# A two-layer encoder step on one core: slot releases by halves, reordered loads around the expert stages, and a rearranged start

## The reference, cut to what matters

```python
# layer 0
h = rms_norm(x, g)
proj = h @ w_in                    # 3072 columns + 8 forget columns
fox = softmax attention over 8 heads x 64, logits + cumulative log_sigmoid(forget)
ret = retention, 4 heads (dk 64, dv 128), rotary on q and k, decay per chunk
x = x + concat(fox, silu(gate) * head_norm(ret)) @ w_out
x = x + moe(rms_norm(x, g))
# layer 1
u = glu(rms_norm(x, g) @ w_pw1)    # 2048 columns
y = silu(layer_norm(causal_depthwise_conv31(u)))
x = x + y @ w_pw2
x = x + moe(rms_norm(x, g))
# moe: top 1 of 4 groups, top 2 of its 8 experts; 32 experts of 1024 -> 256 -> 1024
out = sum over experts e of gate[e] * ((silu(x @ Wg[e]) * (x @ Wu[e])) @ Wd[e])
```

## Time and profile before

| what | value |
|---|---|
| median of 3 runs | 1074.38 us (1073.68 to 1078.66) |
| the profiled execution's own time, its span | 1076.05 us, 1074.2 us |
| TensorE busy over the span | 81% |
| DMA moved | 271.45 MB, mean 253 GB/s |
| expert loads | 192 x 1024 KB, median 22.8 us from issue to landing |
| x_feat | 2 x 768 KB |
| x_tok, first w_in unit | 1536 KB, 1024 KB |
| small, mixc, cst, rcst | 484.5, 196, 918, 1030 KB |
| hist | 960 KB |

### The profile page before, as it was taken

One profiled execution on the slowest core, in us unless ns is written; L12 is line 12 of the kernel. 1 busy time (PEld: TensorE's weight loads), 2 busy tenths in 40 slices (PEclk: granted clock), 3 DMA queues, 4 the chain that ended last, 5 costly groups with the idle time before them and its releaser, 6 DMA issues.

```text
span 1074.2 us, 13791 instructions
## 1 busy us (share of the span) xinstructions
PE 875.3 (81%) x5350; PEld 509.5 (47%) x5350; DVE 323.0 (30%) x784; ACT 208.2 (19%) x442; POOL 86.0 (8%) x97
## 2 busy tenths in 40 slices
PE   5799989899579987788732999968958987877882
PEld 4688878688533333233212555536853332332321
DVE  0422542432411111011013388892142110110113
ACT  3222233412201110110112122233120111101100
POOL 0000000000001110110010000000000111111101
PEclk9899989699688999999975999988969999999996
DMA  9421713106946999999995211133234999999965
GB/s 384 195 79 66 211 74 125 40 1 249 423 190 274 417 419 419 419 419 419 401 393 232 79 55 49 58 101 156 86 137 170 380 419 419 419 420 419 413 277 200
DMA packets 47138, 271.45 MB, mean 253 GB/s; under 512 B 10929, under 2 KB 11081, under 8 KB 18073
## 3 DMA queue, kind: packets, MB, share of 16 engines
q1 hardware_dynamic: 33264, 239.64, 54.9%
q0 software_dynamic: 12176, 24.63, 6.7%
q10 hardware_dynamic: 1632, 6.29, 1.5%
HBM read 268.64 MB, written 25.37 MB: 274 GB/s over the span
## 4 chain that ended last, share of the span: by engine, by line
PE 44%; DMA 32%; DVE 5%; issue 2%; ACT 2%; SPq 0%; ACTq 0%; POOLq 0%; DVEq 0%
DMA slot<-in_experts 25%; PE PS L1037 8%; PE PS L948 8%; PE PS L816 6%; PE PS L971 6%; DMA XGT<-rows,IDX 3%; PE PS L563 3%; PE PS L793 2%; DMA outs<-Y,IDX 2%; DMA slot<-outs 2%; PE PS L929 2%; PE PS L1054 2%; PE PS L873 1%; PE PS L919 1%; DVE X L1364 1%
## 5 line engine op out<-in xcount | busy, mean ns | idle before, releaser
L948 PE MATMUL PS<-slot,XG 128*64 128x512 f32 x1024 | 244.1, 623 | 68.0 <-DMA slot<-in_experts 68.0
L948 PEld LDWEIGHTS PS<-slot,XG 128*64 128x64 f32 x1024 | 78.3, 143 | 212.7 <-issue 194.8
L563 PE MATMUL PS<-slot,HT 128*128 128x256 f32 x576 | 136.2, 394 | 11.5 <-DMA slot<-in_w_in 11.0
L1650 DVE SCALAR_TENSOR_TENSOR hid_by_token<-PS,SC,SG 128x256 f32<-128x256 f32 x32 | 15.5, 484 | 400.6 <-ACT SG L1268 400.6
L563 PEld LDWEIGHTS PS<-slot,HT 128*128 128x128 f32 x576 | 111.7, 198 | 29.7 <-DMA slot<-in_w_in 11.0
L971 PE MATMUL PS<-slot,HID 128*64 128x512 f32 x512 | 118.4, 605 | 2.4 <-ACT HID L1273 2.4
L1037 PE MATMUL PS<-HC,slot 128*128 128x384 f32 x256 | 86.0, 491 | 1.6 <-DVE HC L1737 1.6
L1268 ACT ACTIVATE SG<-PS,SC 128x256 f32<-128x256 f32 x32 | 15.2, 475 | 305.3 <-PE PS L948 305.3
L1037 PEld LDWEIGHTS PS<-HC,slot 128*128 128x128 f32 x256 | 47.6, 190 | 40.1 <-issue 9.6
L495 POOL DMA_INDIRECT XGT<-rows,IDX x36 | 36.7, 1019 | 342.9 <-DVE SC L1643 310.2
L1282 ACT ACTIVATE Y<-PS,SC 128x1024 f32<-128x1024 f32 x32 | 35.7, 1114 | 146.8 <-PE PS L971 139.1
(11 more groups left out here) (280 smaller groups left out, 804.7 us busy)
## 6 DMA issues: line engine op xcount, KB each, us to landing
slot<-in_experts SPq DMA_DIRECT2D x192, 1024.0 KB, 22.8
slot<-in_w_in SPq DMA_DIRECT2D x12, 1024.0 KB, 12.0
slot<-in_w_pw SPq DMA_DIRECT2D x12, 1024.0 KB, 8.4
slot<-outs ACTq DMA_DIRECT2D x6, 1024.0 KB, 10.3
slot<-in_w_out SPq DMA_DIRECT2D x4, 1024.0 KB, 5.0
rows<-X POOLq DMA_DIRECT2D x6, 512.0 KB, 7.8
KTC<-in_k_past POOLq DMA_DIRECT2D x1, 2048.0 KB, 13.3
slot<-in_v_past SPq DMA_DIRECT2D x2, 1024.0 KB, 8.3
```

The source lines that it names most:

```text
L563: last = mm(PS[:, 6 + n % 2, 0:UCOL], HT[:, k, P * t:P * (t + 1)], w[:, k, :], start=k == 0, stop=k == KD - 1)
L948: last = mm(PS[CAP * e:CAP * (e + 1), 2 + p % 2, :], XG[:, p % 2, k, CAP * e:CAP * (e + 1)], w[:, 2 * FE * (k % 4):2 * FE * (k % 4 + 1)], ...
```

## The change

Part by part:

- **Start.** SP loads the gains (the first 32 columns of `small`) first, then x_feat and the first w_in unit in four quarters in turn, then x_tok as three tiles, mixc, unit 1, cst. POOL loads the rest of `small` after the last x_tok tile has landed. Scaling of HT waits by quarter. The first Sqrt table load comes before the data. Pieces 0 to 3 have four PSUM banks (6, 7, 0, 1).
- **Retention.** DVE rotates the three tiles before it waits for the logarithm and computes LF.
- **Releases.** `gu_done` counts halves of gate/up, and a pair of gate and up slots is released at the half that used it.
- **Last pair.** For pair 15, `down` of pair 14 stands between the two halves of gate/up, and ACT's Y copy of pair 14 before the silu of pair 15.
- **Convolution loads.** Units 4 and 5 of w_pw1, and so all that is behind them on SP, also wait until the last token tile's expert outputs have landed.
- Some semaphores are merged (`tile_moved0` to `2` for x_tok, outs and y; `xf_in` for first loads).

```diff
         def _(sp):
-            for i in range(2):
-                sp.dma_start(HT[:, 4 * i:4 * i + 4, :], a["x_feat"][:, 4 * i:4 * i + 4, :]).then_inc(S(f"xf_in{i}"), 16)
+            sp.dma_start(small[:, 0:4 * KD], a["small"][:, 0:4 * KD]).then_inc(S("xf_in0"), 16)
+            for i in range(4):
+                sp.dma_start(HT[:, 2 * i:2 * i + 2, :], a["x_feat"][:, 2 * i:2 * i + 2, :]).then_inc(S(f"xf_in{i}"), 16)
+                cols = slice(2 * UCOL * i, 2 * UCOL * (i + 1))
+                sp.dma_start(slot[0][:, cols], a["w_in"][0, :, cols]).then_inc(S(f"xf_in{i}"), 16)
+            for t in range(NT):
+                sp.dma_start(X[:, t, :], a["x_tok"][:, t, :]).then_inc(S(f"tile_moved{t}"), 16)
+            sp.dma_start(mixc[:, :], a["mixc"]).then_inc(S("mix_in"), 16)
...
-            for i in range(N_A):
+            for i in range(1, N_A):
...
-                if i == 0:
-                    sp.dma_start(X[:, :, :], a["x_tok"]).then_inc(S("x_in"), 16)
-                    sp.dma_start(mixc[:, :], a["mixc"]).then_inc(S("mix_in"), 16)
+                if i == 1:
                     sp.dma_start(cst[:, :], a["cst"]).then_inc(S("cst_in"), 16)
...
-                past(sp, "gu_done" if q % 6 < 4 else "d_done", b + (q // 6 + 1))
+                if q % 6 < 4:
+                    sp.wait_ge(S("gu_done"), b * 2 + (2 * (q // 6) + q % 6 // 2 + 1))
+                else:
+                    sp.wait_ge(S("d_done"), b + (q // 6 + 1))
...
                 if i < 2:
-                    sp.wait_ge(S("gu_done"), b1 - 1)
+                    sp.wait_ge(S("gu_done"), b1 * 2 - 2)
+                elif i < 4:
+                    sp.wait_ge(S("gu_done"), b1 * 2)
                 elif i < LO:
-                    sp.wait_ge(S("gu_done" if i < 4 else "d_done"), b1)
+                    sp.wait_ge(S("d_done"), b1)
+                    sp.wait_ge(S(f"tile_moved{NT - 1}"), 32)
...
         def _(pool):
-            pool.dma_start(small[:, :], a["small"]).then_inc(S("small_in"), 16)
-            pool.wait_ge(S("x_in"), 16)
+            pool.wait_ge(S(f"tile_moved{NT - 1}"), 16)
+            pool.dma_start(small[:, 4 * KD:], a["small"][:, 4 * KD:]).then_inc(S("small_in"), 16)
...
+            def in_bank(n):
+                return (6, 7, 0, 1)[n] if n < 4 else 6 + n % 2
...
-                    if n >= 2:
-                        pe.wait_ge(S("pj_ready"), n - 1)
+                    if n >= 4:
+                        pe.wait_ge(S("pj_ready"), n - 3 if n < 6 else n - 1)
...
-                    if p >= 2:
+                    if p >= 2 and half == 0:
                         pe.wait_ge(S("hidT_ready"), b + (p - 1))
-                    for k in range(KD):
+                    for k in range(4 * half, 4 * half + 4):
...
                     for p in range(NP):
-                        gate_up(b, u, p)
+                        gate_up(b, u, p, 0)
+                        if p == NP - 1:
+                            down(b, u, p - 1)
+                        gate_up(b, u, p, 1)
...
-                        if p >= 1:
+                        if 1 <= p < NP - 1:
                             down(b, u, p - 1)
...
                     for p in range(NP):
+                        if p == NP - 1:
+                            y_out(b, u, p - 1)
                         silu(b, u, p)
-                        if p >= 1:
+                        if 1 <= p < NP - 1:
                             y_out(b, u, p - 1)
...
+            act.wait_ge(S("one_ready"), 1)
+            q.link(A(stat[:, 13:14], stat[:, 15:16], ACT.Sqrt))
             for k in range(0, KD, 2):
-                act.wait_ge(S(f"xf_in{k // 4}"), 16)
+                act.wait_ge(S(f"xf_in{k // 2}"), 32 if k > 1 else 48)
...
             ts(FF[:, :, :], FF[:, :, :], 0.0, None, ALU.min)
-            dve.wait_ge(S("ff_ln"), 1)
-            tt(LF[:, :, :], FF[:, :, :], LT[:, :, :], ALU.subtract, S("lf_ready"))
...
             for t in range(NT):
                 dve.wait_ge(S("pj_ready"), NT + t + 1)
                 rotate(t)
+            dve.wait_ge(S("ff_ln"), 1)
+            tt(LF[:, :, :], FF[:, :, :], LT[:, :, :], ALU.subtract, S("lf_ready"))
```

More of the change, by code:

```diff
@@ L441, in _ @@
                 sp.wait_ge(S("x_done"), NT + t + 1)
-                sp.dma_start(o["y"][:, t, :], X[:, t, :]).then_inc(S("y_stored"), 16)
-            sp.wait_ge(S("y_stored"), 16 * NT)
+                sp.dma_start(o["y"][:, t, :], X[:, t, :]).then_inc(S(f"tile_moved{t}"), 16)
+            for t in range(NT):
+                sp.wait_ge(S(f"tile_moved{t}"), 64)
         @block.gpsimd
         def _(pool):
-            pool.dma_start(small[:, :], a["small"]).then_inc(S("small_in"), 16)
-            pool.wait_ge(S("x_in"), 16)
+            pool.wait_ge(S(f"tile_moved{NT - 1}"), 16)
+            pool.dma_start(small[:, 4 * KD:], a["small"][:, 4 * KD:]).then_inc(S("small_in"), 16)
             pool.dma_start(rcst[:, :], a["rcst"]).then_inc(S("ret_in"), 16)
@@ L545, in full @@
                 before = N_A // LO if seg == "c" else 0
-                pe.wait_ge(S(f"full{i % LO}"), 16 * (before + i // LO + 1))
+                first = 1 if i % LO == 0 else 0
+                pe.wait_ge(S(f"full{i % LO}"), 16 * (before + i // LO + 1 - first))
             pieces = iter(range(NT * N_IN))
+            def in_bank(n):
+                return (6, 7, 0, 1)[n] if n < 4 else 6 + n % 2
             def dense_in(m):
@@ L555, in dense_in @@
                     w = dense(pos)
-                    if t == 0:
+                    if t == 0 and n:
                         full("a", pos)
-                    if n >= 2:
-                        pe.wait_ge(S("pj_ready"), n - 1)
+                    if n >= 4:
+                        pe.wait_ge(S("pj_ready"), n - 3 if n < 6 else n - 1)
                     for k in range(KD):
@@ L562, in dense_in @@
                             pe.wait_ge(S("ht_odd" if k % 2 else "ht_even"), k // 2 + 1)
-                        last = mm(PS[:, 6 + n % 2, 0:UCOL], HT[:, k, P * t:P * (t + 1)], w[:, k, :], start=k == 0,
+                        last = mm(PS[:, in_bank(n), 0:UCOL], HT[:, k, P * t:P * (t + 1)], w[:, k, :], start=k == 0,
                                   stop=k == KD - 1)
@@ L936, in full_pair, with gate_up @@
                     pe.wait_ge(S(f"ex_full{q % SLOTS // 2}"), u * (32 * LAPS) + (32 * (q // SLOTS) + 32))
-                def gate_up(b, u, p):
-                    if p >= 2:
+                def gate_up(b, u, p, half):
+                    if p >= 2 and half == 0:
                         pe.wait_ge(S("hidT_ready"), b + (p - 1))
-                    for k in range(KD):
+                    for k in range(4 * half, 4 * half + 4):
                         if k % 4 == 0:
@@ L1110, in rms @@
                 q.settle()
-                q.link(A(norms[:, n, 3 + t0:3 + t1], norms[:, n, t0:t1], ACT.Sqrt, scale=1.0 / D, bias=C["eps"]),
-                       S("rms_ready"))
-            act.wait_ge(S("small_in"), 16)
+                q.link(A(norms[:, n, 3 + t0:3 + t1], norms[:, n, t0:t1], ACT.Sqrt, scale=1.0 / D,
+                         bias=C["eps"] if n else stat[:, 14:15]), S("rms_ready"))
+            act.wait_ge(S("one_ready"), 1)
+            q.link(A(stat[:, 13:14], stat[:, 15:16], ACT.Sqrt))
             for k in range(0, KD, 2):
-                act.wait_ge(S(f"xf_in{k // 4}"), 16)
+                act.wait_ge(S(f"xf_in{k // 2}"), 32 if k > 1 else 48)
                 q.do(A(HT[:, k, :], HT[:, k, :], ACT.Copy, scale=GC[:, 0, k:k + 1]), S("ht_even"))
-            act.wait_ge(S("x_in"), 16)
             for t in range(NT):
+                act.wait_ge(S(f"tile_moved{t}"), 16)
                 square(0, t, HN[:, t, :])
-            act.wait_ge(S("cst_in"), 16)
             rms(0, 0, NT)
@@ L1377, in rstd @@
                 q.link(V.reciprocal(norms[:, n, 6 + t0:6 + t1], norms[:, n, 3 + t0:3 + t1]), S("rstd_ready"))
+            q.do(V.memset(stat[:, 14:15], EPS))
+            q.do(V.memset(stat[:, 15:16], 1.0), S("one_ready"))
+            for k in range(1, KD, 2):
+                dve.wait_ge(S(f"xf_in{k // 2}"), 32 if k > 1 else 48)
+                q.do(V.tensor_scalar(HT[:, k, :], HT[:, k, :], GC[:, 0, k:k + 1], None, ALU.mult), S("ht_odd"))
+            rstd(0, 0, NT, 1)
             dve.wait_ge(S("small_in"), 16)
-            for k in range(1, KD, 2):
-                dve.wait_ge(S(f"xf_in{k // 4}"), 16)
-                q.do(V.tensor_scalar(HT[:, k, :], HT[:, k, :], GC[:, 0, k:k + 1], None, ALU.mult), S("ht_odd"))
             for lay in range(2):
                 tt(WR[:, lay, :, :], WR[:, lay, :, :], bc(GC[:, 2 * lay + 1, :], 2, NR), ALU.mult, S("wr_ready"))
-            rstd(0, 0, NT, 1)
             ts(GQ[0:FD, :], GQ[0:FD, :], FD ** -0.5, None, ALU.mult, sem=S("gq_ready"))
@@ L1655, in rows_out @@
                     if p >= 2:
-                        dve.wait_ge(S("gu_done"), b + (p - 1))
+                        dve.wait_ge(S("gu_done"), b * 2 + (2 * p - 2))
```

14 lines of the change are left out of this document (8 added, 6 removed).

## The result

The changed kernel takes 1034.47 us (median of 4 runs, 1031.48 to 1038.82) against 1074.06: a ratio of 0.9627, 95% interval 0.9602 to 0.9651. The forecast was 1037, with 39 us of gain from the profiled execution; the medians lie 39.6 apart. The profiled execution of the changed kernel is the fastest of its runs: 1031.48 us, span 1029.6.

What follows compares the result with a forecast made beforehand. TensorE was taken to bound attention and convolution, DMA weight streaming both expert stages. Gains 14.1 + 6.3 + 16.4 + 2.9 - 0.8 = 38.9 us from 1076.05 gave 1037.1, median 1035.5; forecast 1037, range 1029 to 1050.

Steps and rivals of the forecast that it cites:

- Start: First loads and pieces: quarters and four PSUM banks end the first three pieces at 18.5 instead of 24.2 us, gain 5.7.
- data flows as if from 3.4 us on: First loads: at 415 GB/s from 3.4 us, the first quarter lands at 5.0 us and the fourth at 9.8.
- Rival B: First loads: the quarters pay their fixed time one by one, up to 0.9 us each, +7 us, 1044; chance 0.12.
- Rotation: Before the attention part: rotating ahead of LF removes TensorE's 6.89 us idle and the lower clock behind it, gain 8.4 us.
- Releases by halves: Restart of the expert weight streams: earlier loads and gather gain 6.3 us in layer 0, 2.9 in layer 1, nothing inside the stream.
- End of layer 0: Last pair and the loads behind it: last scatter leaves at 549.7, last addition ends at 567.9 against 584.3, gain 16.4 us.
- Rival C: End of layer 0's experts: contention stays because units 0 to 3 still load, gain 8 instead of 16.4, 1045; chance 0.15.
- End of layer 1: Last pair of layer 1's experts: the reordered down costs 0.8 us (0 to 2).
- The second half waited only 0.24 us (1040.57), so the moved down of 3.65 stands in its way: Layer 1's last gate/up: the moved down delays it instead of covering the activation, 1055.8 against 1054.96.
- Rival D: Expert streams: shorter, more frequent waits keep TensorE at 1.2 GHz; 1081 at x = 0.36, 1100 at x = 0.45; chance 0.03.
- Rival E: The gathers still come late, or the start idles elsewhere: 10 us less gain, 1047; chance 0.08.
- The signs: Trace checks: first products near 6 us, no rotation or gather waits, release inside gate/up, 108 us convolution; last quarter after 12 us refutes.

Runs made afterwards that it cites:

- again: The changed kernel run once more with no edit, timed against the kernel before: 1037.46 us, ratio 0.9656.
- no_quarters: The changed kernel with the first loads as before (features in two halves, first weight unit whole, `small` first, `cst` ahead of unit 1): 1039.14 us, ratio 0.9665.
- no_rot: The changed kernel with LF and its wait for the logarithm moved back in front of the rotations: 1045.47 us, ratio 0.9735.
- no_half: The changed kernel with gate and up slots released only at the end of a whole gate/up pass, as before: 1043.62 us, ratio 0.9719.
- no_behind: The changed kernel without the wait for the last expert outputs ahead of convolution units 4 and 5: 1052.28 us, ratio 0.9807.
- no_last: The changed kernel with the last pair in the old order in both layers, ScalarE's Y copy behind the silu again: 1038.52 us, ratio 0.9666.

## Why the prediction was right

**The sum.** 38.9 us were forecast; the profiled execution shows 44.6, of which 5.1 are the attention part's clock. That had no term and deserved none: it is a draw that every execution makes anew. Without it 39.5 are left, and `again`, which has the long low stretch there as the kernel before has, leads by 38.6. The medians give 39.6, and 36.3 in the set of `again`. Several terms were off and cancel, and that they cancel this well is luck.

**Start: 5.7 forecast, 3.5 found.** The failing step is the line "data flows as if from 3.4 us on" at 415 GB/s. It was drawn from transfers with 6 and 8 KB in a row of a partition; the quarters have 3 and 2 KB and flow at 223 to 304 GB/s up to 8 us, so the fourth quarter was used at 11.7 instead of 9.8. With the old first loads the rate is 425 GB/s again (`no_quarters`), so the new ones cost it. The undone parts return 1.2 to 2.4 us for the quarters and 0.4 to 1.7 for the banks. Rival B had the sign of this right and the size wrong: 0.9 us for each transfer is out. A cost of some 0.24 us each would fit the 1.9 us that the last of the quarters is late, with eight transfers more than before, but number, size and rows of the transfers changed together, and no run separates them.

**Rotation: 8.4 forecast, 9.6 found, 8.2 to 9.4 returned by `no_rot`.** Idle and clock, as described. The full length of a transpose group was read from rows of another form (128\*128 in the earlier trace rows, 128\*64 here); the trace has 1.04 us for eight of them, so the 1.1 holds.

**Releases by halves: 6.3 and 2.9 forecast, 5.9 and 1.6 found, 4.6 to 5.3 and 3.1 to 4.1 returned by `no_half`.** The gather wait shrank to 0.70 and 0.51 us instead of zero, and layer 1's first gate/up took 8.69 us instead of 7.90, more of it at the lower clock. Layer 1's old row was a lucky one: no clock was lost behind its wait of 2.95 us, while in `no_half` a wait of 2.43 us lost some. In the stream nothing changed, as forecast.

**End of layer 0: 16.4 forecast, 17.5 found** (16.6 and 0.9 ahead of it). The attribution was less good than the number. I let the last scatter's earlier leave (554.05 to 549.7) count for 4.4 us by itself. `no_behind` has that leave and no gain at all, `no_last` keeps 14.5 us without it. The loads behind are the main cause, and the reorder pays (3 us) only once they are gone. Rival C is out: units 2 and 3 held back as well bring 1.8 us.

**End of layer 1: a loss of 0.8 forecast, a gain of 1.9 found.** Most of the 1.9 is the clock: the first half of the last pair ran at the lower clock before and at the full clock in the changed kernel.

```profile
1034.98 5.35 PE L948 MATMUL PS<-slot,XG 128*64 128x512 f32 x16 [2.76 <-DMA slot<-in_experts]
```

The failing step is "The second half waited only 0.24 us (1040.57), so the moved down of 3.65 stands in its way". It priced a row of the lower clock. At the full clock the second half waits 1.27 us, the down fits in, and the reorder gains 0.7 to 1.1 us. At the lower clock the step itself holds, but its size does not: old and new order lie within 0.4 us of each other. Down and second half follow each other in 3.43 us where 3.65 were added up, and the exposed chain was 2.1 us where 2.4 were estimated.

**Rival D** (a low clock in the streams, 0.03): the granted clock stays high between its dips of 3.4 to 6.8 us, and the streams are 0.9 and 1.9 us shorter, not longer. Its price at x = 0.45 was added up wrongly: by its own formula it is 35 us a layer and 1108, not 1100. Rival E (10 us less) is out by the waits of 0.70 and 0.51 us and a start 2.2 us short of its term.

**The signs.** SyncE's first release is at 288.01, inside the first gate/up (282.82 to 291.3); nothing waits before the rotation's transposes; the last scatter is not behind another; TensorE is busy 107.38 of the 108 us from 547 us on, so no wait for units 4 or 5. The first product came at 7.30 instead of near 6, the gathers are still waited for a little, and from the last scatter to the last addition it is 18.5 us instead of 16 to 18. The last quarter at 11.7 lies just inside the 12 that would have spoken against the forecast.

## What to carry to other kernels

Look in a stage bound by transfers for the moments when its queue runs dry: a release half a pass earlier was worth 3 to 5 us there and nothing in the full stream. Loads that nobody needs yet, queued ahead of short transfers on the critical path, can cost most of their own length: here 8.4 MB, an estimated 20 us of the queue at the 415 GB/s of the earlier trace rows, cost 14.5 to 17.4 us, and one wait on the sequencer that issues them gave that back. Before pricing a wait from one row, and before crediting a microsecond to an edit, look at the clock of the instruction ahead of it in both traces.

## What the runs showed of the hardware

The same program ran the attention part's low-activity stretch with 6.8 or up to 20.5 us at the lower clock, which moved the length of that part by 5.4 us. At the start of the program, transfers with rows of 2 and 3 KB kept the DMA engines 0.86 to 0.98 busy at 223 to 225 GB/s, and the same kind of rows went at 414 GB/s from 8 to 10 us; with rows of 6 and 8 KB the same microseconds show 425 GB/s. Why the first microseconds are slower with the split transfers stays open.
